# A two-layer decoder step on one core: the gate projection as seven products of halved blocks, with the output products placed behind the up tiles

## The reference

```python
def swiglu(x, w_in, w_out):
    gate, up = jnp.split(x @ w_in, 2, axis=-1)
    return (jax.nn.silu(gate) * up) @ w_out

x = x + 0.5 * swiglu(rms_norm(x, p['ffn1_norm']), p['ffn1_w_in'], p['ffn1_w_out'])
...                      # attention, recurrence, convolution, x = x + merged @ w_out
x = x + 0.5 * swiglu(rms_norm(x, p['ffn2_norm']), p['ffn2_w_in'], p['ffn2_w_out'])
```

## Time and profile before

| | |
|---|---|
| median of three runs | 2886.69 us (2882.81 to 2886.81) |
| profiled execution, its own time | 2886.48 us |
| its span, first to last instruction | 2884.8 us |
| PE busy | 2829.6 us (98%), 21280 matmuls |
| DVE busy | 1693.6 us (59%) |
| ACT busy | 1112.6 us (39%) |
| POOL busy | 312.8 us (11%) |
| chain that ended last | PE 93%, DVE 3%, ACT 1% |

### The profile page before, as it was taken

The page is one execution under the profiler, slowest core; times in us unless marked ns, Lnnn a source line. Parts: engine busy times, 40 slices in busy tenths (PEclk is TensorE's granted clock), DMA queues, the critical chain, the costliest instruction groups (busy, mean ns, idle before and its releaser), DMA issues.

```text
span 2884.8 us, 56179 instructions
## 1 busy us (share of the span) xinstructions
PE 2829.6 (98%) x21280; PEld 2764.3 (96%) x21280; DVE 1693.6 (59%) x2441; ACT 1112.6 (39%) x1669; POOL 312.8 (11%) x232
## 2 busy tenths in 40 slices
PE   7999999999999999999999999999999999999999
PEld 6999999899999999999999999998889999999998
DVE  4564756676655446656556565576666445575654
ACT  4332423555522333333333333335554223333324
POOL 1121201000000111111102021100000001030301
PEclk9999999999999999999999999999999999999999
DMA  3222223333222222222222223233332222222222
GB/s 121 73 88 87 88 74 99 90 96 87 82 80 87 89 85 70 95 73 97 80 76 87 88 73 103 74 89 90 90 107 71 87 80 97 74 81 95 73 88 91
DMA packets 299060, 249.22 MB, mean 86 GB/s; under 512 B 20643, under 2 KB 296307, under 8 KB 298919
## 3 DMA queue, kind: packets, MB, share of 16 engines
q1 hardware_dynamic: 296775, 242.44, 27.2%
q0 software_dynamic: 2144, 4.98, 0.5%
HBM read 240.04 MB, written 7.34 MB: 86 GB/s over the span
## 4 chain that ended last, share of the span: by engine, by line
PE 93%; DVE 3%; issue 1%; ACT 1%; DVEq 1%; DMA 0%; POOLq 0%; ACTq 0%; SPq 0%
PE ps L509 74%; PE ps L549 11%; PE ps L709 1%; PE ps L648 1%; PE ps L647 1%; PE ps L649 1%; PE ps L774 1%; PE ps L727 1%; PE ps L689 1%; DVE bl L1258 1%; DVE tmp L1223 1%; DVE wlo L1249 1%; PE ps L696 0%; PE ps L711 0%; DMA xin<-in_x_sample 0%
## 5 line engine op out<-in xcount | busy, mean ns | idle before, releaser
L509 PE MATMUL ps<-hh,whi 128*128 128x288 f32 x4480 | 965.3, 297 | 11.5 <-DVE wlo L1217 5.0
L509 PE MATMUL ps<-hl,whi 128*128 128x288 f32 x4480 | 959.3, 296 | 0.0
L509 PE MATMUL ps<-hh,wlo 128*128 128x288 f32 x4480 | 959.2, 296 | 0.0
L873 ACT ACTIVATE whi<-wraw 128x1024 fp32r<-128x1024 f32 (+1 forms) x388 | 403.9, 1042 | 1162.5 <-PE ps L509 1136.0
L509 PEld LDWEIGHTS ps<-hh,whi 128*128 128x128 f32 x4480 | 722.0, 189 | 14.2 <-DVE wlo L1217 5.9
L509 PEld LDWEIGHTS ps<-hh,wlo 128*128 128x128 f32 x4480 | 722.1, 189 | 0.0
L509 PEld LDWEIGHTS ps<-hl,whi 128*128 128x128 f32 x4480 | 721.9, 189 | 0.0
L1217 DVE TENSOR_TENSOR wlo<-wraw,whi 128x1024 fp32r<-128x1024 f32 (+1 forms) x388 | 467.0, 1204 | 374.4 <-ACT whi L873 373.6
L1266 DVE TENSOR_TENSOR tmp<-tmp,ps 128x576 f32<-128x576 f32 x128 | 96.6, 754 | 344.9 <-PE ps L509 344.5
L549 PE MATMUL ps<-bh,whi 128*128 128x288 f32 x896 | 266.8, 298 | 18.3 <-ACT tmp L956 12.8
L549 PE MATMUL ps<-bl,whi 128*128 128x288 f32 x896 | 264.3, 295 | 0.0
(11 more groups left out here) (333 smaller groups left out, 3549.9 us busy)
## 6 DMA issues: line engine op xcount, KB each, us to landing
wraw<-in_ffn_w_in SPq DMA_DIRECT2D x88, 1024.0 KB
wraw<-in_ffn_w_out SPq DMA_DIRECT2D x32, 1024.0 KB
wraw<-in_w_in SPq DMA_DIRECT2D x28, 1024.0 KB
wraw<-in_w_in SPq DMA_DIRECT2D x56, 512.0 KB
wraw<-in_ffn_w_out SPq DMA_DIRECT2D x16, 768.0 KB
wraw<-in_w_branch SPq DMA_DIRECT2D x24, 512.0 KB
wraw<-in_w_out SPq DMA_DIRECT2D x9, 1024.0 KB
kv<-in_cache_k SPq DMA_DIRECT2D x128, 64.0 KB, 1.8
```

The lines of the kernel that those rows point to most:

```text
L509: last = pe.matmul(ps[slot][:, half, 0:HF], weights, rhs[:, k, half * HF:(half + 1) * HF], start=(start and c == 0 and n == 0), stop=(stop ...
L873: act.activation(split_tile(into, j, rowwise), raw_tile(slot, j, rowwise), ACT.Copy).then_inc(hi_ready, 1)
```

## The change

The three parts and their loops are replaced by one list of units, written out in full for each feed-forward block. There are 11 steps `s` of two hidden chunks. A step is one up unit (plain tiles) and then one gate unit. The gate unit is now seven products too, over the 8 input chunks, with four chunk halves per piece. The output products of steps 0 and 1 (4 chunks), 2 to 4 (6 chunks) and 5 to 7 (6 chunks) stand between the up unit and the gate unit of steps 2, 5 and 8; their pieces have two or three chunk halves instead of four. Steps 8 to 10 keep plain output tiles at the end.

All weight pieces go through one ring of four half pieces: when PE has finished piece `i`, ACT and DVE split the piece that stands four later (`BEHIND`). POOL makes four sums for each of the 23 seven-product units of a block, before for 8.

The gate unit needs sums of blocks of the normed input, `th` and `tl`. They are made by DVE and ACT at three places: at the start of the kernel, behind the mixer's output tiles, and behind the last output tiles of the second feed-forward block, for the next layer (`norm_sums`; also after the last layer). `past_forgets` now stands behind the whole first feed-forward block and the two loads of the stage `fv`, and waits until that block's last tile is filled.

```diff
+def ffn_units():
+    units = []
+    for s in range(STEPS):
+        units.append(("up", s, 0))
+        if s in (2, 5, 8):
+            units += [("out", s // 3, v) for v in range(4)]
+        units.append(("gate", s, 0))
+    return units + [("last", 3, v) for v in range(4)]
...
-        for pairs in (4, 4, 3):
-            s[name].append((Stage(plan, pairs, 2, 4), Stage(plan, 2, 2, 4), 2 * pairs))
+        s[name] = Stage(plan, 1, len(FFN_UNITS), 2 * len(FFN_UNITS))
...
             def past_forgets(L):
 
-                norm = S["ffn1norm"]
-                wait_apart(sp, filled[norm.slot(0)], norm.turn(0, L) + 1)
+                st, k = S["ffn1"], 2 * len(FFN_UNITS) - 1
+                wait_apart(sp, filled[st.slot(k)], st.turn(k, L) + 1)
...
                 for k in range(2):
                     load(fv, k, L, 0, ("w_in", 0, KD, COL_V + 256 * k, 256))
+                past_forgets(L)
...
+            def buffers_free(st, f, n, L):
+                kind, s, v = FFN_UNITS[n]
+                if kind == "out" and v == 0:
+                    act.wait_ge(mov_ready, blocks_ready(L, f, PART_STEPS[s][-1], 4))
+                elif kind == "gate" and FFN_UNITS[n - 1][0] == "out":
+                    act.wait_ge(freed[st.slot(2 * n - 2)], st.turn(2 * n - 2, L) + 1)
+                elif kind == "gate" and 0 < s <= 8:
+                    act.wait_ge(mov_ready, blocks_ready(L, f, s - 1, 4))
+                elif kind == "gate" and s > 8:
+                    act.wait_ge(a_ready, L * 12 + (6 * f + 2 * (s - 8)))
...
+                    for m in range(7 if n in SEVEN_NO else 4):
+                        wait_done(act, st, f, i, L)
+                        if n in SEVEN_NO and m in (0, 1, 2, 4):
+                            parts(st, f, n, m, L)
+                        for j in BEHIND[i]:
+                            ring_split(st, f, j, L)
...
+            def even_sums(c, g):
+                dve.tensor_tensor(tmp[4][:, 0:HF], x[:, c, HF:N], x[:, c, 0:HF], ALU.subtract)
+                dve.tensor_scalar(tmp[4][:, HF:N], x[:, c, HF:N], g, None, ALU.mult)
...
+            def kept_whole(c, raw):
+                dve.drain()
+                dve.tensor_copy(two(ah[:, c, :]), raw)
+                dve.drain()
+                dve.tensor_tensor(two(al[:, c, :]), raw, two(ah[:, c, :]).bitcast(F32), ALU.subtract).then_inc(a_ready, 1)
...
+            def gate_part(st, f, n, i, m, L):
+                first, second = ps[st.slot(2 * n)], ps[st.slot(2 * n + 1)]
+                norm, pf = tmp[6], tmp[5]
+                s = FFN_UNITS[n][1]
+                if m == 3:
+                    wait_tile(st, 2 * n + 1, L)
+                    dve.wait_ge(part_copied, copied(L, f, n, 3))
+                    dve.tensor_tensor(kept[:, 1, :], kept[:, 1, :], second[:, 0, 0:HF], ALU.add).then_inc(freed[st.slot(2 * n + 1)], 1)
+                elif m == 5:
+                    wait_done(dve, st, f, i, L)
+                    dve.tensor_tensor(kept[:, 0, :], kept[:, 0, :], first[:, 1, 0:HF], ALU.add)
+                    dve.drain()
+                    dve.tensor_tensor(kept[:, 0:2, :], kept[:, 0:2, :], two(norm[:, 0:N]), ALU.mult).then_inc(gate_in, 1)
+                    dve.wait_ge(part_copied, copied(L, f, n, 4))
+                    dve.tensor_tensor(pf[:, HF:N], pf[:, HF:N], tmp[2][:, 0:HF], ALU.add)
+                elif m == 6:
+                    dve.drain()
+                    wait_tile(st, 2 * n, L)
+                    dve.tensor_tensor(pf[:, 0:HF], norm[:, 0:HF], first[:, 0, 0:HF], ALU.mult).then_inc(freed[st.slot(2 * n)], 1)
+                    dve.tensor_tensor(pf[:, HF:N], pf[:, HF:N], norm[:, HF:N], ALU.mult).then_inc(gate_in, 1)
...
             first_weights(1)
+            for c in range(KD):
+                if c % 2 == 0:
+                    even_sums(c, gains[:, 0, c:c + 1])
+                else:
+                    odd_sums(c, gains[:, 0, c - 1:c], gains[:, 0, c:c + 1])
+                    norm_sums_lo(0, c // 2)
...
+                        elif kind == "last" and m % 2:
+                            if v == 3:
+                                split_ahead(st, k, L)
+                            if f == 0:
+                                norm_next(L, c, 8, L, 8)
                             else:
+                                norm_next(L, c, 24, L + 1, 0)
+                                norm_sums(L, L * 16 + 16, c, L + 1, 0)
```

More of the change, by code:

```diff
@@ new lines, in parts @@
+            def parts(st, f, n, m, L):
+                kind, s, v = FFN_UNITS[n]
+                first, second = ps[st.slot(2 * n)], ps[st.slot(2 * n + 1)]
+                if kind == "out":
+                    one, other = scratch(v)
+                    places, scale = (one[:, 0:HF], other[:, HF:N], one[:, HF:N], None, other[:, 0:HF]), 0.5
+                else:
+                    places, scale = (kept[:, 0, :], tmp[5][:, HF:N], kept[:, 1, :], None, tmp[2][:, 0:HF]), 1.0
+                if m == 0:
+                    buffers_free(st, f, n, L)
+                src = second[:, 0, 0:HF] if m == 1 else first[:, 0, 0:HF]
+                act.activation(places[m], src, ACT.Copy, scale=scale).then_inc(part_copied, 1)
@@ L1018, in _ @@
             first_weights(1)
+            for kk in range(4):
+                norm_sums(0, kk)
             act.wait_ge(pre_done, 2)
@@ L1750, in weight_sums @@
                         pool.drain()
+                    last = n
             add_squares(0)
             with pool.Fori(0, DEPTH) as L:
-                for part in range(2):
-                    weight_sums(S["ffn1"][part][1], part_no(0, part), L)
+                weight_sums(S["ffn1"], 0, L)
                 add_squares(L * 24 + 8)
@@ L1794, in _ @@
                 add_squares(L * 24 + 16)
-                for part in range(2):
-                    weight_sums(S["ffn2"][part][1], part_no(2, part), L)
+                weight_sums(S["ffn2"], 1, L)
                 add_squares(L * 24 + 24)
```

707 lines of the change are left out of this document (387 added, 320 removed).

## The result

The changed kernel takes 3030.44 us (median; 3028.46 to 3039.63) against 2886.33 us on the same chip: 1.0508 times as long, with an interval of 1.0485 to 1.0531. The forecast was 2871 us with a range up to 2918, so the direction was wrong and the time lies 112 us above the range. The profiled execution has a span of 3028.6 us, 143.8 more than before.

What follows compares the result with a forecast made beforehand. PE's matmuls were taken to set the time, at 133 ns each. A gain of 92.4 us less the added costs summed to -15.5, from 2886.48 to 2871 us; range 2840 to 2918 for 8 in 10 runs.

Steps and rivals of the forecast that it cites:

- the tight point is the step from up to gate: Gate unit's start: ACT's first copy waits for DVE's last block; 0.2 us for 44 units, 9 us, ends 0 and 31.
- sums that fall into it: Gate unit: POOL's sums beside DVE's 8.4 us; four a pair add 3.1, giving DVE 19.9 us for PE's 24.0.
- The clock: Kernel start: first matmuls after PE's long idling run at the lower clock, 1.3 us more.
- Rival three: Gate and output units: POOL's sums hold DVE; 2917 us at a 75% share, decides from about 62%; chance 0.22.
- Outputs in small pieces: Output units: DVE ends after PE, 15 us for pieces of 6 matmuls, 4 us for pieces of 9.
- first units: First output unit of each of 12 stages: same wait as the gate, 0.5 us on average, 6 us, ends 3 and 15.
- Start: Kernel start: PE waits 17.9 us for the first split instead of 2.75; 16.5 us in all, ends 10 and 19.
- Cache table: Later DMAs make `lf` ready after PE asks: 2.5 us in each layer, 5 us, ends 0 and 10.
- Last tiles: Each block's last output tiles: PE waits 2.6 us for hidden chunks, four times, 10.4 us, ends 6 and 16.
- End: Kernel end: input sums and two ACT copies queued ahead of the output copies, 4 us, ends 1 and 7.
- Layer turn: Between the layers: input sums make DVE leave late; with the last stage 7 us, ends 0 and 12.
- the rule on two readers of SBUF: Two-input DVE instructions and GpSimd instructions reading SBUF exclude each other; the later waits for the other's whole length.

Runs made afterwards that it cites:

- e13: Changed kernel with POOL's weight sums left out in the gate units alone, those of the output units kept: 2897.59 us, 1.0037.
- e5: Changed kernel with ACT's copies waiting block by block, and those of a step's first blocks moved behind the next up unit's first item: 2915.17 us, 1.0104.
- e7: e5 with POOL's weight sums replaced by writes of four values: 2860.14 us, 0.9908.
- e8: e5 with the cache table's 16 DMAs back inside the first feed-forward block, ahead of its last output weights' loads: 2905.37 us, 1.0067.
- e10: Changed kernel with POOL only writing constants, nearly as long as the sums took, and signalling each sum afterwards: 2864.28 us, 0.9924.

## Why the prediction was wrong

- **The step that failed** is "the tight point is the step from up to gate": "DVE's last block of the step before, which comes 2.0 to 3.3 us after the up unit's end", and from it "0.2 us for 44 units, 9 us". Measured: 6.1 us after the gate unit's start with the sums, 2.2 without, at the gate unit worked out above, and 32 waits of 2.5 us on average, 80.1 us. Of these only 20, 52.9 us, are waits for the last block. The other 12, 27.2 us, are waits for DVE's last addition into `x` of an output unit, and the prediction had no such wait: it took all 44 gate units as one kind. The end of the chain was summed with one hold (split "0.68 to 1.78"), but three more sums lie upstream on the same chain, between the last products of the gate unit and its second silu (2.76 us), and nothing downstream takes them up. I had put them down as "sums that fall into it" and checked only that DVE's 19.9 us of work fit in 24.0 of PE. They do fit; DVE idles for 3.75 us of the late gate unit.
- **The clock** was priced at the start alone (1.3 us; 12 slow matmuls there, right) and nowhere else, since I forecast no other long pause. The low clock brought 51 us, some 35 of them behind the 21 waits on `kept` that slow matmuls follow, the rest at the other pauses. The 80 us of stalls, 36 of low clock and 7 of restarts are the 123 us that e13 got back, beside its closer matmuls.
- **Rival three** named the right mechanism and place, with a chance of 0.22, but its price and its turning point were wrong. It made the cost grow with the share of POOL's time that lands on DVE, "decides from a share of about 62%". The share was 48%, under my 55%, and the time still came out 113 us over its 2917.
- **Outputs in small pieces**: 15 for steps 0 and 1, 4 for the others, 6 for first units, 25 in all. In e5, where the gate units behind up units no longer wait, the stages with output products cost 4 x 7.9 + 8 x 3.0 = 56 us, some 19 of them in the gate unit behind the products; without the sums (e7) 4 x 2.6, 10 us, since the stages of steps 5 and 8 then run at full rate. The 25 was too low by about half, for the same reason: with POOL's sums gone 46 of the 56 us go. The 192 sums of the output units alone cost 36 us by e13.
- **Seams.** Start: 16.5 forecast; PE waited 20.54 us instead of 2.75, and 12 slow matmuls, 19. Cache table: 5 forecast, 7.4 of waits, 10 by e8. Last tiles: 10.4 forecast, 8.3 on `al`. End: 4 forecast, 7.5 where 1.2 stood. Layer turn: 7 forecast; waits of 1.4, 4.2 and 3.3 us where one of 1.65 stood, and some 30 more slow matmuls, 10 to 11 us. All inside or at the ends that I gave.
- **Right**: 528 matmuls and 133 ns, 11.2 us for a gate unit that nothing holds, the rule on two readers of SBUF. Gate units of 12 us or more were named as the sign for rival three, and the profile shows them: 13.2 to 17.3 us in steps 1 to 8.

## What to carry to other kernels

When work is added to an engine that contends with another, do not only compare the two engines' totals in a stretch. Write down the chain of instructions from the last product of one unit to the operand that the next unit needs, with every operation that may fall beside a contending one, compare its length with the moment of need, and add all holds on it to one sum: here 3.85 us of hold against 0.6 us of margin at the gate unit that was worked out, and waits of 1.8 to 3.2 us at 32. Then ask what a wait asks for: one that wants everything at the first product makes the last instruction of the chain the deadline for all, and taking it by block was worth 100 us for a few lines.

## What the runs showed of the hardware

- POOL's additions of two SBUF operands lengthened DVE's two-input instructions beside them by 0.83 to 1.09 us in the four pairs shown; POOL's writes of constants in e10, 400 us in all, do not (689 ns for a 512-wide split with them and without any).
- A pause of PE of 2 to 3.2 us may or may not bring the lower clock: behind 3.19 us at 180.98 the matmuls start 0.13 us apart, behind 3.17 us at 299.61 they start 0.24 us apart for several microseconds. All eight pauses of 2.05 us are followed by 15 slow matmuls each, and eleven others, of 1.8 to 3.2 us, by one or none, so the length of the pause alone does not decide. The same wait in a kernel thus costs unequal amounts, which a price per wait does not show; the count of slow matmuls does.
